# Two feed-forward second phases: earlier loads and splits of the first pairs, the norm's affine part on VectorE, and the last pairs in two steps

## What is computed

```python
def _swiglu(h, w13, w2):
    a = h @ w13                                   # 1024 -> 2 x 2816
    return (jax.nn.silu(a[..., :D_FF]) * a[..., D_FF:]) @ w2

def _ffn_sublayer(x, shift, scale, gate, w13, w2, g, b):
    y = _swiglu(_modulate(x, shift, scale), w13, w2)
    return _layer_norm(ALPHA * x + FFN_RES * gate * y, g, b)
```

## Time and profile before

| | us |
|---|---|
| median of 3 runs | 2442.62 |
| lowest, highest | 2438.69, 2444.28 |
| the profiled execution | 2443.89 |
| its span in the profile | 2442.1 |
| TensorE busy | 2292.4 (94%) |
| VectorE busy | 1372.3 (56%) |
| ScalarE busy | 807.1 (33%) |
| POOL busy | 247.4 (10%) |

### The profile page before, as it was taken

One profiled execution on the slowest core, in us unless ns is written; L12 is line 12 of the kernel. 1 busy time (PEld: TensorE's weight loads), 2 busy tenths in 40 slices (PEclk: granted clock), 3 DMA queues, 4 the chain that ended last, 5 costly groups with the idle time before them and its releaser, 6 DMA issues.

```text
span 2442.1 us, 31717 instructions
## 1 busy us (share of the span) xinstructions
PE 2292.4 (94%) x12172; PEld 1967.1 (81%) x12186; DVE 1372.3 (56%) x2272; ACT 807.1 (33%) x1371; POOL 247.4 (10%) x204
## 2 busy tenths in 40 slices
PE   7999999999999998798899988979999999999996
PEld 7888888888788887797789877867878888877885
DVE  4676666666345365335542454754766665638735
ACT  3522222222243244422234224641633333323331
POOL 0000000000000000160000003520000000007303
PEclk9999999999999999899999999989999999999998
DMA  7153344353464454041000001031322233245552
GB/s 260 37 153 108 100 120 135 116 152 117 164 240 159 147 165 127 26 130 35 18 18 18 18 1 44 10 99 23 112 78 77 77 91 90 77 175 170 164 167 83
DMA packets 197851, 250.45 MB, mean 103 GB/s; under 512 B 13606, under 2 KB 145118, under 8 KB 197726
## 3 DMA queue, kind: packets, MB, share of 16 engines
q1 hardware_dynamic: 197726, 248.73, 32.3%
HBM read 208.05 MB, written 40.63 MB: 102 GB/s over the span
## 4 chain that ended last, share of the span: by engine, by line
PE 76%; DVE 11%; ACT 4%; DMA 4%; issue 2%; POOL 1%; SPq 1%; DVEq 0%; ACTq 0%; POOLq 0%
PE psum L1131 10%; PE psum L1132 10%; PE psum L1133 10%; PE psum L551 6%; PE psum L553 6%; PE psum L552 6%; DMA raw<-in_ffn_w 3%; PE psum L1580 2%; PE psum L1581 2%; PE psum L1582 2%; PE psum L1965 2%; PE psum L1151 2%; PE psum L1150 2%; PE psum L1149 2%; PE psum L1573 1%
## 5 line engine op out<-in xcount | busy, mean ns | idle before, releaser
L1131 PE MATMUL psum<-x_mix_h,x_op_h 128*128 128x512 f32 x640 | 250.6, 392 | 4.8 <-DVE v_sum L974 4.8
L1132 PE MATMUL psum<-x_mix_l,x_op_h 128*128 128x512 f32 x640 | 250.0, 391 | 0.0
L1133 PE MATMUL psum<-x_mix_h,x_op_l 128*128 128x512 f32 x640 | 249.5, 390 | 0.0
L884 ACT ACTIVATE x_op_h<-raw 128x512 fp32r<-128x512 f32 x140 | 86.0, 628 | 215.7 <-PE psum L1133 129.0
L884 ACT ACTIVATE x_op_h<-w_sum 128x512 fp32r<-128x512 f32 x160 | 97.6, 625 | 159.0 <-DVE w_sum L862 85.2
L1131 PEld LDWEIGHTS psum<-x_mix_h,x_op_h 128*128 128x128 f32 x640 | 120.7, 189 | 29.3 <-DVE x_op_l L890 5.3
L1133 PEld LDWEIGHTS psum<-x_mix_h,x_op_l 128*128 128x128 f32 x640 | 120.4, 188 | 25.4
L1132 PEld LDWEIGHTS psum<-x_mix_l,x_op_h 128*128 128x128 f32 x640 | 120.8, 189 | 23.5
L1226 POOL TENSOR_TENSOR ln_stats<-ln_stats,consts 128x1 f32<-128x1 f32 x26 | 16.8, 647 | 1194.9 <-DVE ln_stats L1221 1194.9
L890 DVE TENSOR_TENSOR x_op_l<-raw,x_op_h 128x512 fp32r<-128x512 f32 x140 | 92.8, 687 | 42.8 <-ACT x_op_h L884 40.4
L551 PE MATMUL psum<-w_0h,g_h 128*128 128x512 f32 x256 | 102.0, 398 | 13.6 <-DVE g_l L537 13.6
(11 more groups left out here) (378 smaller groups left out, 6090.3 us busy)
## 6 DMA issues: line engine op xcount, KB each, us to landing
raw<-in_ffn_w SPq DMA_DIRECT2D x198, 512.0 KB, 4.7
ada_slice<-in_w_ada SPq DMA_DIRECT2D x56, 512.0 KB, 3.9
f_rows<-g_out SPq DMA_DIRECT2D x88, 256.0 KB, 2.6
p_raw<-in_w_in SPq DMA_DIRECT2D x22, 512.0 KB, 4.8
g_raw_a<-f_rows SPq DMA_DIRECT2D x44, 256.0 KB, 3.7
early<-in_w_ada SPq DMA_DIRECT2D x16, 512.0 KB, 6.6
y<-in_x SPq DMA_DIRECT2D x16, 512.0 KB, 8.4
x_rows<-y SPq DMA_DIRECT2D x16, 512.0 KB, 3.2
```

Source lines behind the costliest of these rows:

```text
L884: nc.scalar.activation(op_tiles(F, op)[0][:], OP_SOURCE[op], ACT.Copy).then_inc(F.hi, 1)
L1131: nc.tensor.matmul(o, wh[:, k], high(k), start=i < 4 and k == 0, stop=False, skip_group_check=i > 3)
L1132: nc.tensor.matmul(o, wh[:, k], low(k), start=False, stop=False, skip_group_check=i > 3)
L1133: last = nc.tensor.matmul(o, wl[:, k], high(k), start=False, stop=k == KH - 1, skip_group_check=i > 3)
```

## The change

What it does, in the order of the diff (F1's and F2's analogous hunks are shown once):

- Loads of each pair 1 to 10 wait for the stores of that pair's own blocks (`stored_by`) instead of pair 1's for all. Pair 1 uses the first `g_raw` buffer, as pair 0.
- In F2's second chunk, the first two units multiply pairs 8 and 9 of the chunk before TensorE waits for the last pair; then these units take the last pair, and the other units all three.
- From block 9 of F1 on, four slices of `w_ada` a block in eight blocks (two at the third place) and none in the last three.
- SP issues pair 1's loads in the last block, behind the store of the block before and ahead of the last block's own stores. In the last block pair 0's high parts come before the first silu and its low parts after the second of the sums of products. F1's residual rows wait for the last product at the head of `second1_sp`.
- F1's unit 2 waits for the first silu of the last block.
- `x2_pool` is gone: VectorE multiplies and adds two tiles after each of pairs 5 to 8. ScalarE no longer takes part in F2's last norm, and POOL only raises to -0.5; VectorE does the rest in two instructions a tile, (y - mean) x gain and then x inverse deviation + bias. For tiles 0 to 3 this comes after pairs 12 to 15, for the others right after their statistics. The last tile is done and stored in halves.

```diff
@@ -394,6 +394,10 @@
                 self.y_read = sem(name + "_y_read")
                 self.y_added = sem(name + "_y_added")
 
+            def stored_by(self, P_, k):
+
+                return (self.stored_before + self.n if k < 2 else 0) + 2 * P_
+
             def units(self, c):
                 return 2 * len(self.groups[c])
 
@@ -482,9 +486,9 @@
 
             c, p = divmod(P_, PAIRS)
             at, size = F.column[F.groups[c][0]], P * len(F.groups[c])
-            if P_ == 1:
+            if 0 < P_ < PAIRS:
                 for k in range(F.n):
-                    sp.wait_ge(g_stored[k], 16 * F.stored[k])
+                    sp.wait_ge(g_stored[k], 16 * F.stored_by(P_, k))
             for i in range(2):
                 f = 2 * p + i
                 sp.wait_ge(F.lo, item(F, P_ - 1, i, 0) + 1 if P_ else F.free[i])
@@ -497,7 +501,7 @@
             return F.w2_first if P_ == 0 else w2_ring[(P_ - 1) % 3]
 
         def g_raw_of(F, P_):
-            return F.g_raw[int(P_ > 0)]
+            return F.g_raw[int(P_ > 1)]
 
         def g_slot(F, P_):
             return F.g_first if P_ == 0 else (g_h[P_ % 3], g_l[P_ % 3])
@@ -563,9 +567,14 @@
                         bank_free(u)
                     done = second_unit(pe, F, c, u, [p])
                 done.then_inc(F.pair_done, 1)
+            head = 2 if F.merged[c] == 3 else 0
+            if head:
+                pe.wait_ge(F.lo, item(F, c * PAIRS + PAIRS - 2, 1, 1) + 1)
+                for u in range(head):
+                    second_unit(pe, F, c, u, range(F.plain(c), PAIRS - 1))
             pe.wait_ge(F.lo, item(F, c * PAIRS + PAIRS - 1, 1, 1) + 1)
             for u in range(F.units(c)):
-                second_unit(pe, F, c, u, range(F.plain(c), PAIRS)).then_inc(F.y_ready, 1)
+                second_unit(pe, F, c, u, range(F.plain(c) if u >= head else PAIRS - 1, PAIRS)).then_inc(F.y_ready, 1)
                 after_unit(u)
 
         def evacuate_dve(dve, F, N, c, t, row):
@@ -654,7 +663,11 @@
         VECTORS = [2, 2, 2] + [1] * (MODS_LATE - 3)
         SLICES = [(g, k) for g in range(MODS_LATE) for k in range(KD)]
         SLICE_PLAN = [[8 * (j // 3) + 3 * (j % 3) + i for i in range(3 if j % 3 < 2 else 2)] for j in range(9)]
-        SLICE_PLAN += [[s for s in range(24 + 3 * j, 27 + 3 * j) if s < len(SLICES)] for j in range(QUICK - 9)]
+        SLICE_PLAN += [list(range(24 + 4 * j, 28 + 4 * j)) if j < 8 else [] for j in range(QUICK - 9)]
+
+        def slices_at(j, place):
+            return SLICE_PLAN[j][place:place + 1 if place < 2 else None]
+
         assert sorted(sum(SLICE_PLAN, [])) == list(range(len(SLICES)))
 
         def slice_ops(s):
@@ -707,7 +720,7 @@
 
         def complete(j, place):
 
-            return [SLICES[s][0] for s in SLICE_PLAN[j][place:place + 1] if SLICES[s][1] == KD - 1]
+            return [SLICES[s][0] for s in slices_at(j, place) if SLICES[s][1] == KD - 1]
 
         def first_high(act, F):
             for i in range(2):
@@ -914,6 +927,8 @@
                     second_loads(sp, F, 0)
                 if j:
                     quick_stored(sp, F, j - 1, 1)
+                if j == QUICK - 1:
+                    second_loads(sp, F, 1)
                 ahead = sum(len(p) for p in SLICE_PLAN[:j + 1])
                 for s in range(loaded, min(ahead + 1, len(SLICES))):
                     slice_sp(sp, s)
...
@@ -999,13 +1016,13 @@
                 keep_product(act, F, j)
                 if ahead:
                     quick_high(act, F, j + 1, ("A11", "A21", "S2", "S1", "S3"))
+                else:
+                    act.wait_ge(ada_used, MODS_LATE)
+                    second_high(act, F, 0)
                 silu_first(act, F, j)
                 silu_ctx(act, F, j)
                 if ahead:
                     quick_high(act, F, j + 1, ("A12", "A22"))
-                else:
-                    act.wait_ge(ada_used, MODS_LATE)
-                    second_high(act, F, 0)
                 silu_second(act, F, j)
                 if ahead:
                     quick_high(act, F, j + 1, ("S4",))
...
@@ -1038,14 +1055,14 @@
                 quick_sum(dve, F, v_sum[:], 3, v_sum[:], 2, 4, j)
                 if ahead:
                     quick_low(dve, F, j + 1, ("S3",))
+                else:
+                    second_low(dve, F, 0)
                 slices(j, 2)
                 quick_sum(dve, F, F.X.c_sum, 3, u_sum[:], 1, 6, j)
                 gated(dve, F, 0, F.X.c_sum, j, 4)
                 gated_ctx(dve, F, j)
                 if ahead:
                     quick_low(dve, F, j + 1, ("A12", "A22"))
-                else:
-                    second_low(dve, F, 0)
                 last_sum(dve, F, j)
                 gated(dve, F, 1, v_sum[:], j, 3)
                 if ahead:
...
@@ -1306,10 +1323,9 @@
 
         def second1_sp(sp):
 
-            for P_ in range(1, 3 * PAIRS):
+            sp.wait_ge(F1.ab_ready, F1.products)
+            for P_ in range(2, 3 * PAIRS):
                 second_loads(sp, F1, P_)
-                if P_ == 2:
-                    sp.wait_ge(F1.ab_ready, F1.products)
                 if P_ in (2, 3):
                     for t in ROWS1[5 * P_ - 10:5 * P_ - 5]:
                         sp.dma_start(y[:, t, :], token_rows(t)).then_inc(rows_back, 16)
@@ -1327,6 +1343,8 @@
             def first_free(u):
                 if u == 0:
                     pe.wait_ge(mod_ready, MODS_LATE + 2)
+                if u == 2:
+                    pe.wait_ge(F1.sig_ready, F1.n * (FB - 1) + 1)
                 if u == 4:
                     pe.wait_ge(F1.glu_ready, F1.n * FB)
 
@@ -2596,20 +2614,19 @@
                         turn_pe(pe, T3, T3_BANKS, norm2_done, (0, k))
 
 
-        out_last = sem("out_last")
         out_affined = sem("out_affined")
-
-        def x2_pool(pool):
-
-            pool.wait_ge(x2_gains_in, 32)
-            pool.wait_ge(rows_back, 16 * (TA + TL))
-            for t in range(TL):
-                nc.gpsimd.tensor_tensor(y[:, t, :], y[:, t, :], ln_rows_x2[:, 0], ALU.mult).then_inc(x2_affined, 1)
-                pool.wait_ge(x2_affined, 2 * t + 1)
-                nc.gpsimd.tensor_tensor(y[:, t, :], y[:, t, :], ln_rows_x2[:, 1], ALU.add).then_inc(x2_affined, 1)
+        out_stats = place("out_stats", 200, [P, TL, 18])
+
+        def x2_rows_dve(dve, t):
+
+            if t == 0:
+                dve.wait_ge(x2_gains_in, 32)
+                dve.wait_ge(rows_back, 16 * (TA + TL))
+            step(dve, nc.vector.tensor_tensor(y[:, t, :], y[:, t, :], ln_rows_x2[:, 0], ALU.mult))
+            nc.vector.tensor_tensor(y[:, t, :], y[:, t, :], ln_rows_x2[:, 1], ALU.add).then_inc(x2_affined, 1)
 
         def last_sp(sp):
-            for P_ in range(1, 2 * PAIRS):
+            for P_ in range(2, 2 * PAIRS):
                 second_loads(sp, F2, P_)
                 if P_ == 2:
                     sp.wait_ge(F2.ab_ready, F2.products)
@@ -2620,54 +2637,67 @@
                 if P_ == PAIRS:
                     for i, src in enumerate((ln_g[0, 2:3, :], ln_b[0, 2:3, :])):
                         sp.dma_start(ln_rows3[:, i], src.to_broadcast([P, D])).then_inc(x2_gains_in, 16)
+            for t in range(TL - 1):
+                sp.wait_ge(out_affined, t + 1)
+                sp.dma_start(out_rows[t], y[:, t, :]).then_inc(out_done, 16)
+            for half in range(2):
+                cols = slice(half * BANK, (half + 1) * BANK)
+                sp.wait_ge(out_affined, TL + half)
+                sp.dma_start(out_rows[TL - 1][:, cols], y[:, TL - 1, cols]).then_inc(out_done, 16)
+            sp.wait_ge(out_done, 16 * (TL + 1))
+
+        def last_pool(pool):
+
             for t in range(TL):
-                if t < TL - 1:
-                    sp.wait_ge(out_affined, 2 * t + 2)
-                else:
-                    sp.wait_ge(out_last, 2)
-                sp.dma_start(out_rows[t], y[:, t, :]).then_inc(out_done, 16)
-            sp.wait_ge(out_done, 16 * TL)
-
-        def last_pool(pool):
-
-            pool.wait_ge(x2_gains_in, 64)
-            for t in range(TL):
-                norm_pool(pool, N3, t)
-                if t:
-                    affine_out(pool, nc.gpsimd, t - 1, out_affined, t - 1)
+                pool.wait_ge(N3.measured, t + 1)
+                nc.gpsimd.tensor_tensor(out_stats[:, t, 16:17], out_stats[:, t, 14:15], minus_half[:, 0:1], ALU.pow)\
+                    .then_inc(N3.inverted, 1)
 
         def last_act(act):
-            for P_ in range(1, PAIRS + 1):
+            for P_ in range(1, 2 * PAIRS):
                 second_high(act, F2, P_)
-            for t in range(3):
-                norm_act(act, N3, t, t)
-            second_high(act, F2, PAIRS + 1)
-            norm_act(act, N3, 3, 3)
-            for P_ in range(PAIRS + 2, 2 * PAIRS):
-                second_high(act, F2, P_)
-            for t in range(4, TL):
-                norm_act(act, N3, t, t)
-
-        def affine_out(engine, ops, t, done, before):
```

(41 more changed lines are left out.)

13 lines of the change are left out of this document (7 added, 6 removed).

## The result

| | before | after |
|---|---|---|
| median | 2440.65 us (4 runs) | 2404.24 us (4 runs) |
| lowest, highest | 2438.55, 2444.28 | 2400.45, 2405.76 |
| the profiled execution | 2443.89 | 2400.45 |
| its span | 2442.1 | 2398.3 |

The ratio is 0.9849 (95% interval 0.9832 to 0.9866): the change saves 36.4 us. The same kernel timed again in the experiments (`full`) gave 2404.08 us and 0.9853 (0.9837 to 0.9869). Where these 5.4 us come from is the subject of this part.

The account below looks back on a forecast made before the run. TensorE's matmuls were taken as the bound, so only its second-phase idle time, the slow clock after it and the tail could pay: 7.3 + 20.6 + 6.4 = 34.3 us, 2443.89 - 34.3 = 2409.6 us, range 2404 to 2419.

Parts of the forecast that it names:

- the basis: Whole kernel: the profiled execution's 2443.89 us, from which the summed gain was subtracted; 1.3 us above the median then known.
- part 5: Behind the last matmul: 16.2 us shrinks to 9.2 to 9.4, plus 0.4 for GpSimd's power; gain 6.4 us, bounds 5 to 7.
- the last half's store: End of the tail: 3.1 us, between 3.3 seen for a whole row and an estimated 2.5.
- GpSimd's power: Last tiles: the power of -0.5 takes 0.65 us on GpSimd and makes VectorE's first half wait 0.4 us.
- Part 1: Start of F1's second phase: earlier modulation, pair 0 parts and pair 1 loads remove waits; gain 7.3 us, bounds 5.7 to 7.4.
- Parts 2 and 3: F2's chunk 0: earlier pair 0 parts and pair 1 loads, x2's affine part on VectorE; gain 12.9 us.
- part 4: F2's last three pairs: two units put first cover the 4.75 us wait and 2.1 us slow clock; chunk 1's gain 7.7 us.
- the sign of being right: End of the kernel: 9 to 10 us behind the last matmul, among the signs that would show the forecast right.
- Load chain stays the bound: Second phases: bursts of y rows don't move or pair 1 is late; 5 to 9 us less gain, 2415 to 2419; chance 0.15.
- VectorE the bound of the end: Last tiles: affine instructions of 2.3 us make a tile 9.3 us for TensorE's 8.16; 2416 us; chance 0.10.
- The change doesn't do what it says: Last blocks: pair 0's early parts wait for loads and hold VectorE's sums; gain only 22 us, 2421; chance 0.02.
- A slower clock in the long unbroken run: Second phases: TensorE's clock falls to a mean of 0.935 or less over some 515 us; 2445 us and up; chance 0.02.

Follow-up runs that it names:

- three_slices: The full change, with three slices a block from block 9 to the end as before; 2410.54 us, ratio 0.9884.
- x2_alone: The kernel before, with only x2's affine rows moved from GpSimd to VectorE; 2434.11 us, ratio 0.9984.
- tail_alone: The kernel before, with only the final norm's new form and its stores; 2432.8 us, ratio 0.997.
- late_parts: The full change, with pair 0's high and low parts back behind the last block's other work in both phases; 2410.66 us, ratio 0.9876.
- late_loads: The full change, with pair 1's loads back behind the last block's last store in both phases; 2412.45 us, ratio 0.9891.
- x2_on_pool: The full change, with x2's affine rows back on GpSimd; 2410.44 us, ratio 0.987.
- no_head: The full change, with no unit ahead of the last pair in F2's second chunk; 2413.92 us, ratio 0.9897.
- wide_beside: The full change, with an added, unused GpSimd instruction of 128x512 behind the power in each of the last four rows; 2406.97 us.

## Why the prediction was right in kind, and which of its terms were wrong

Each part, undone or done alone, showed at the place that the forecast named. The time didn't come out as forecast, and what was wrong are two terms of the sum. The step that failed first is the basis, the 2443.89 us of the one profiled execution in "2443.89 - 34.3 = 2409.6": the kernel before measured 2440.65 us in the median, so 3.2 of the 5.4 us were there before any part was priced. The second is part 5, the tail, forecast to save 6.4 us where 7.3 were measured: the last half's store took 2.5 us for 3.1, and GpSimd's power held VectorE 0 to 0.13 us for 0.4. By its own steps:

- **Part 1, F1's start: right.** 7.3 us forecast, 7.3 between the two profiles. Pair 4 was the tight one, ready within 0.2 us of the forecast, with 0.3 us to spare. The fourth slice costs TensorE nothing that shows: it has no wait in the quick phase of `full`, and that phase took 505.2 us with four slices and 505.6 with three (`three_slices`, its wait left out). One caution on the size: the untouched code of F1's second phase took 306.6 us in the forecast's profile, but 309.8 in `x2_alone` and 307.4 in `tail_alone`, with longer `g_l` waits (3.7 and 2.9 us instead of 2.2) and a slow clock behind one of them in each, while the changed kernel took 298.9 or 299.3. The profile that the forecast was made on was the cheapest of the three. Over these three executions the gain is 8.8 in the mean, so that 7.3 met 7.3 is in part luck.
- **Parts 2 and 3, F2's chunk 0, and part 4: right.** 20.6 us forecast, 20.7 measured. Each stall returned when its part was undone: 2.33 us before pair 0 (`late_parts`), 0.86 before pair 1 (`late_loads`), three before later pairs (`x2_on_pool`), 4.74 before the last (`no_head`).
- **Part 5, the tail: right in kind, its term mis-sized.** 6.4 us forecast, 7.3 measured (7.3 also alone). Two terms were too large. The larger error is the store of the last half: 3.1 us was taken, 2.5 came (2395.82 to 2398.3), which is 0.6 of the 0.9 us. The 3.1 leaned on the 3.3 us of a whole row; the 2.5 that the forecast named beside it as an estimate was the right one. The other is the price set for GpSimd's power, "which then waits 0.4 us": it measured nothing beside a whole row and 0.13 us beside the halves. I had carried over the row of two long instructions holding each other up to one of a single column. The rest of the sum held: 3.4 us behind the last unit came as 3.4, and the two pairs of halves took 1.54 and 1.41 us for 1.4 and 1.3. The 8.9 us also lie just under the 9 to 10 that were named as the sign of being right.
- **The basis: wrong.** The sum was subtracted from the profiled execution, 2443.89 us. The kernel before has medians of 2439.65 to 2440.65 in the groups since, 3.2 to 4.2 lower. The forecast said that the median "may lie 1.3 lower" and left the likeliest time at the profile's; it should have been moved to the median of all runs at hand, and even these three were high. 3.2 of the 5.4 us are this, the other 2.1 are the gain: 0.9 from the tail, 0.1 from F2, and the rest, as far as one can tell, from F1's second phase being dearer before than in the one profile. This last piece is worked out from three executions and not shown by one that isolates it, and it is smaller than what the two medians can tell.
- **The Trainium skill's rule,** "SBUF — State Buffer", section "Who interferes with whom", says that a VectorE instruction with two SBUF inputs contends with a GpSimd one that reads SBUF. It calls the ports that the two engines share an exclusive lock, and lets the order of issue decide who blocks. On the long instructions the trace agrees that both are held: in `x2_on_pool` VectorE's low parts of 128x512 took 2.28 us in the mean beside GpSimd's additions of 3.26 us, where they take 0.685 without; in `wide_beside` the GpSimd instruction took 1.82 us where it began 0.68 us before the end of a VectorE instruction, and 1.27 in the last row, and VectorE's next one was held 0.9. What I made of it, that VectorE would wait for the rest of the power's 0.65 us, 0.4 us, the trace does not bear out: 0 and 0.13 us.
- **The rivals.** Load chain stays the bound: no, but the 0.3 us of F1's pair 4 show how near it was, and `late_parts` shows what it looks like (2.50 us). VectorE the bound of the end: no, it waits 0.82 us a tile; with 1.28 us for each affine instruction a tile takes 7.3 us for TensorE's 8.16. The change doesn't do what it says: no. A slower clock in the long unbroken run: no, 1.00 in all of F2's 239.4 us.

## What to carry to other kernels

A stall at one pair can be worth more than its own length: where the buffers of a ring come free decides the loads several pairs later, so follow an edit to the tightest pair (here the fourth, with 0.3 us to spare) and not to its own place. Forecast against the median of the runs, not against the profiled one, and check the size of a gain on the stretches that the change touches. Once they hold no stalls they repeat well (0.4 us in F1's second phase, less in F2's and the tail); a stretch with stalls need not: F1's second phase of the kernel before took 306.6 to 309.8 us. So profile the kernel before more than once too. Where VectorE and GpSimd hold each other up, look first at GpSimd's large instructions: here those of 128x512 and 128x1024 cost VectorE 0.9 us and more each, the one-column ones 0.13 at most.
